# A streaming encoder step on one core: pairwise convolution, tile 0 routed first, its first 16 rows summed by VectorE

## What is computed

```
h = rmsnorm(x); q, k, v, g, a, b = split(h @ w_in)           # six sections of 512 columns
q, k = rotary(q), rotary(k);  o = decayed_retention(q, k, v)  # 4 heads of 128, a state per head
y_ret = silu(g) * normalise(o) * gain
u = a * sigmoid(b); c = depthwise_conv(u, 31 taps) + bias     # 512 channels, over time
y_conv = silu(layernorm(c))
x = x + concat(y_ret, y_conv) @ w_out
h = rmsnorm(x)                                                # then, for each of 8 heads:
scores = (h @ query_head) @ keys      # two halves of 128 keys; top 16 of each, top 16 of the 256 sums
act = gelu(h . down[expert]);  x += sum over 16 experts of softmax * act * up[expert]
y = rmsnorm(x)
```

## Time and profile before

| | us |
|---|---|
| median of 3 runs | 1797.5 |
| the runs | 1796.53, 1797.82, 1797.5 |
| the profiled execution, time | 1796.54 |
| its span, first to last instruction | 1794.6 |
| TensorE, mean granted clock | 0.945 |

### The profile page before, as it was taken

How to read it: one execution, slowest core, us unless ns; L and a number is a source line. 1 busy time by engine, 2 the same in 40 slices (tenths; PEclk the granted TensorE clock), 3 DMA queues, 4 the chain that set the end, 5 groups by cost and what they waited for, 6 DMA issues and landing times.

```text
span 1794.6 us, 14135 instructions
## 1 busy us (share of the span) xinstructions
PE 1522.6 (85%) x4008; PEld 700.3 (39%) x4008; DVE 1171.6 (65%) x2667; ACT 496.4 (28%) x1562; POOL 744.8 (42%) x654
## 2 busy tenths in 40 slices
PE   7999979968988978997798889788977988777887
PEld 3544345534433433342244334333423443332332
DVE  2089863357567767766766777677677677777655
ACT  1000110122332333332333323333333332333332
POOL 1002144133254545453554544444454445455452
PEclk9899989989999999998999999999999999899899
DMA  5112100288999999999999999999999999999996
GB/s 221 47 58 83 62 1 1 68 341 329 362 404 421 421 421 421 422 421 422 421 402 423 422 420 401 422 421 389 408 422 421 421 421 422 421 421 410 421 416 248
DMA packets 84847, 605.53 MB, mean 337 GB/s; under 512 B 10880, under 2 KB 11136, under 8 KB 13088
## 3 DMA queue, kind: packets, MB, share of 16 engines
q0 software_dynamic: 78336, 570.46, 77.1%
q1 hardware_dynamic: 6432, 34.16, 5.0%
HBM read 601.31 MB, written 2.88 MB: 337 GB/s over the span
## 4 chain that ended last, share of the span: by engine, by line
DMA 39%; PE 38%; DVE 13%; ACT 4%; issue 2%; POOL 1%; DVEq 1%; ACTq 1%; POOLq 0%; SPq 0%
DMA arena<-experts,expert 38%; PE ps L1246 21%; DVE region_b L728 6%; PE ps L1217 5%; PE ps L1090 5%; DVE arena L933 5%; PE ps L1077 3%; ACT weight L623 2%; ACT diag L630 1%; PE ps L1082 1%; PE ps L1189 1%; POOL arena L465 1%; PE ps L1104 1%; ACT gl L620 1%; ACTq L625 1%
## 5 line engine op out<-in xcount | busy, mean ns | idle before, releaser
L1246 PE MATMUL ps<-arena,diag 128*128 128x512 f32 x2176 | 1031.2, 631 | 234.1 <-ACT diag L630 233.9
L465 POOL DMA_INDIRECT arena<-experts,expert x544 | 669.3, 1230 | 760.3 <-PE ps L1246 672.4
L933 DVE CUSTOM_DVE_ANT_0 arena<-arena,hn 128x1024 f32<-128x1024 f32 x544 | 654.8, 1222 | 365.9 <-DMA arena<-experts,expert 361.4
L1246 PEld LDWEIGHTS ps<-arena,diag 128*128 128x128 f32 x2176 | 428.8, 201 | 818.9 <-issue 603.4
L620 ACT ACTIVATE gl<-dots 128x4 f32<-128x4 f32 x136 | 27.9, 205 | 801.4 <-DVE dots L933 801.4
L630 ACT ACTIVATE diag<-cst,weight 128x128 f32<-128x128 f32 x544 | 173.8, 390 | 9.6 <-issue 0.3
L1090 PE MATMUL ps<-arena,hT 128*128 128x512 f32 (+1 forms) x320 | 145.9, 616 | 1.0 <-issue 1.0
L623 ACT ACTIVATE weight<-gl,gate 128x1 f32<-128x1 f32 x544 | 115.8, 283 | 9.9 <-issue 0.7
L728 DVE SCALAR_TENSOR_TENSOR region_b<-region_b,par 128x512 f32<-128x512 f32 x240 | 108.0, 521 | 2.7 <-issue 0.5
L1217 PE MATMUL ps<-hT,region_b 128*128 128x512 f32 x224 | 98.5, 593 | 0.4 <-issue 0.4
L441 POOL TENSOR_TENSOR hn<-arena,cst 128x256 f32<-128x256 f32 (+1 forms) x20 | 16.2, 808 | 193.5 <-ACT arena L529 127.0
(11 more groups left out here) (125 smaller groups left out, 845.1 us busy)
## 6 DMA issues: line engine op xcount, KB each, us to landing
arena<-weights SPq DMA_DIRECT2D x8, 2048.0 KB, 8.9
region_b<-head_weights SPq DMA_DIRECT2D x8, 1152.0 KB, 9.4
arena<-experts,expert POOLq DMA_INDIRECT x544, 14.9
xs<-x_prompt SPq DMA_DIRECT2D x4, 512.0 KB, 5.2
y_prompt<-xs SPq DMA_DIRECT2D x4, 512.0 KB, 4.1
cst<-consts SPq DMA_DIRECT2D x1, 836.0 KB, 12.4
region_b<-gain_ffn SPq DMA_DIRECT2D x1, 512.0 KB, 3.7
region_b<-gain_final SPq DMA_DIRECT2D x1, 512.0 KB, 11.5
```

Of the source, the lines that this page charges most:

```text
L465: pool.indirect_dma_start(rows_of(n), None, experts, bass.IndirectOffsetOnAxis(ap=expert[:, vt % BUFS, k:k + 1], axis=0))\
L933: last = v.tensor_tensor_reduce(out=rows_of(n)[:, 0:D], in0=rows_of(n)[:, 0:D], in1=hn[:, tile_of(vt)], scale=1.0, scalar=0.0, op0=ALU.mul ...
L1246: last = mm(ps[:, 2 * (vt % 2) + half, :], diag[:, n % DIAGS, :], rows_of(n)[:, D + half * SEC:D + (half + 1) * SEC], start=k == 0, stop=k ...
```

## The change

Three things are changed. None changes what is computed.

*The convolution by pairs of channel groups.* Prompt and sample columns of a channel group now lie in one row (`EXT` = 604 columns: pad, 512, state of 30, 32), so one instruction covers 574 columns. VectorE does GLU and 31 taps for groups 0 and 1, then for 2 and 3, with two instructions and a drain a tap. TensorE forms the GLU in halves of 272 columns (prompt and sample together), the groups of the first pair first; it begins when three tiles are turned.

*One list, tile 0 first.* `plan()` replaces the two lists and the loops ahead of them. The gate of tile 0 is formed before the channel mean, the other gate tiles and v behind it; layer norm goes in blocks of columns 0 to 128 and 128 to 544; `mix_out`, turn, query and keys of tile 0 come before the retention of tiles 2 to 4 is done. ScalarE evacuates the transposes of q and k and the transposes back. `gate_tanh` has four buffers. GpSimd rotates in place, q and k in one pass of 512 columns, and only behind the last tap. PSUM has eight banks in rotation up to `ffn_t(0, 0)`, and from there banks 4 to 7. SyncE's waits are for products of TensorE instead of a drain behind a section; tile 0's gain has a place of its own.

*The first 16 rows summed by VectorE.* For head tile 0 ScalarE forms only the weights, no diagonals; VectorE adds weight times the `up` half of each row to x (`sum_here`), 16 instructions of 128x1024, each with a drain. Slots get an order of their own (`SLOT`, `PLACE`) for the first 15 gathers: gathers 7 to 10 reuse the slots of 0 to 3, and 11 to 14 take the last weight slots. From gather 26 on each waits for n - 11 as before.

The diff, cut to its core:

```diff
-    for t in range(1, TILES + 1):
-        order += head(t) + out(t - 1) + mid.get(t, []) + scores(t) + back(t - 1) + end.get(t, [])
+    late = [(c, i) for c in (2, 3) for i in range(2)]
+    order = turn("norm_t", 0) + turn("norm_t", 1) + turn("norm_t", 2) + glu(S_A, (0, 0), (1, 0)) + turn("norm_t", 3)
+    order += turn("norm_t", SAMPLE) + glu(S_A, (0, 1), (1, 1)) + glu(S_B, (0, 0), (0, 1), (1, 0), (1, 1))
+    order += glu(S_A, *late) + glu(S_B, *late) + rows(S_Q, *range(TILES)) + rows(S_K, *range(TILES)) + rows(S_G, 0)
+    order += blocks("ln_mean") + rows(S_G, 1) + blocks("ln_var") + rows(S_G, 2, 3, SAMPLE)
+    order += rows(S_V, 0) + head(0) + rows(S_V, 1) + scores(0) + head(1) + out(0) + rows(S_V, 2) + scores(1) + back(0)
+    order += mix(0, 0) + out(1) + head(2) + mix(0, 1) + scores(2) + back(1) + rows(S_V, 3) + turn("ffn_t", 0)
+    order += query(0) + keys(0) + out(2) + head(3) + rows(S_V, SAMPLE) + scores(3) + mix(1, 0) + back(2) + mix(1, 1)
+    order += out(3) + head(4) + scores(4) + turn("ffn_t", 1) + query(1) + keys(1) + back(3) + out(4) + mix(2, 0)
+    order += back(4) + mix(2, 1) + mix(3, 0) + turn("ffn_t", 2) + query(2) + mix(3, 1)
+    order += keys(2) + mix(4, 0) + turn("ffn_t", 3) + query(3) + mix(4, 1) + keys(3)
+    return order + turn("ffn_t", 4) + query(4) + sums(1, 0) + keys(4) + sums(1, 1)
...
-BANKS = 7
+BANKS = 8
+SUM_BANKS = 4
+FIRST_SUM = JOB[("ffn_t", 0, 0)]
+BANK = {name: n % BANKS if n < FIRST_SUM else SUM_BANKS + (n - FIRST_SUM) % (BANKS - SUM_BANKS)
+        for name, n in JOB.items()}
+OPENING = [0, 1, 2, 3, 4, 5, 6, 0, 1, 2, 3, 7, 8, 9, 10]
+CYCLE = [4, 5, 6, 0, 1, 2, 3, 7, 8, 9, 10]
+SLOT = OPENING + [CYCLE[n % SLOTS] for n in range(VT * TOPK - len(OPENING))]
...
+            x_rows(0)
             sp.dma_start(cst[:, C_IDENT:], consts[:, C_IDENT:]).then_inc(s_ident, 16)
             sp.dma_start(par[:, :], params).then_inc(s_par, 16)
+            x_rows(1)
+            x_rows(2)
+            weight_rows(S_A)
...
+            sp.wait_ge(s_pe, JOB[("glu", S_A, CT - 1, 1)] + 1)
+            weight_rows(S_K)
+            sp.wait_ge(s_pe, JOB[("glu", S_B, CT - 1, 1)] + 1)
+            weight_rows(S_G)
+            sp.wait_ge(s_pe, JOB[("qkvg", S_Q, SAMPLE)] + 1)
+            weight_rows(S_V)
...
+            pool.wait_ge(s_conv, 1)
+            rotary(0)
+            decayed_keys(0)
+            for t in range(1, TILES):
+                rotary(t)
...
             mixed_root(0)
+            pool.wait_ge(s_idx, 1)
+            pool.wait_ge(s_pe, JOB[("ret_yT", 1)] + 1)
+            gathers(0, 0, 2)
+            retention_root(2)
+            decayed_keys(3)
+            pool.wait_ge(s_pe, JOB[("qkvg", S_V, SAMPLE)] + 1)
+            gathers(0, 2, 4)
+            pool.wait_ge(s_pe, JOB[("ret_yT", 2)] + 1)
+            gathers(0, 4, 5)
             mixed_root(1)
+            retention_root(3)
+            decayed_keys(4)
+            pool.wait_ge(s_pe, JOB[("ret_yT", 3)] + 1)
+            gathers(0, 5, 6)
+            retention_root(4)
+            pool.wait_ge(s_pe, JOB[("ret_yT", 4)] + 1)
+            gathers(0, 6, 7)
             mixed_root(2)
+            gathers(0, 7, 11)
             mixed_root(3)
+            pool.wait_ge(s_pe, JOB[("mix_out", SAMPLE, 0)] + 1)
+            gathers(0, 11, 13)
+            pool.wait_ge(s_pe, JOB[("mix_out", SAMPLE, 1)] + 1)
+            gathers(0, 13, TOPK)
             mixed_root(SAMPLE)
...
+            for first in range(0, CT, 2):
+                glu(first)
+                last = glu(first + 1)
...
+                for j in range(TAPS):
+                    for c in (first, first + 1):
+                        last = tap(c, j)
+                    if j < TAPS - 1:
+                        dve.drain()
+            last.then_inc(s_conv, 1)
...
+            def sum_here(g):
+
+                for k in range(g * GROUP, (g + 1) * GROUP):
+                    dve.wait_ge(s_diag, k + 1)
+                    v.scalar_tensor_tensor(out=xs[:, 0], in0=rows_of(k)[:, D:2 * D], scalar=weight[:, 0, k:k + 1],
+                                           in1=xs[:, 0], op0=ALU.mult, op1=ALU.add).then_inc(s_used, 1)
+                    dve.drain()
+                if g == GROUPS - 1:
+                    dve.drain().then_inc(s_acc, 1)
...
+            top_sums(0)
+            ret_out(2)
+            ret_state(2)
+            ret_scores(3)
+            mix_add(1, 0)
+            mix_add(1, 1)
+            ret_out(3)
+            ret_state(3)
+            ret_scores(4)
+            dve.wait_ge(s_gain, 16)
             peer_norm(1)
             first_scores(1)
             top_first(1)
+            ret_out(4)
+            ret_state(4)
+            top_second(1)
+            mix_add(2, 0)
+            top_sums(1)
+            mix_add(2, 1)
+
+            gate_scales(0)
+            weigh(0, 0)
+            mix_add(3, 0)
             peer_norm(2)
             mix_add(3, 1)
+            sum_here(0)
+            weigh(0, 1)
             first_scores(2)
             top_first(2)
+            mix_add(4, 0)
+            peer_norm(3)
+            weigh(0, 2)
+            sum_here(1)
             top_second(2)
+            mix_add(4, 1)
             top_sums(2)
             weigh(0, 3)
+            sum_here(2)
+            peer_norm(4)
+            first_scores(3)
 
             gate_scales(1)
             weigh(1, 0)
-            first_scores(3)
+            sum_here(3)
             top_first(3)
             weigh(1, 1)
-            add(0)
```

760 lines of the change are left out of this document (401 added, 359 removed).

## The result

The changed kernel takes 1781.95 us (median of five runs, 1780.23 to 1785.97) against 1796.5 us for the kernel before, timed in the same rounds: a ratio of 0.9924, with the interval 0.9907 to 0.994. The change is worth about 14 us. The prediction said 1756.5 and a range of 1744 to 1777, so it had the sign right and was 25 us too fast, outside its range. The profiled execution took 1783.14 us for a span of 1781.3.

The account below looks back on a forecast made before the run. The prediction took a front until the first later_query, then a DMA-bound stretch of constant length, as the bound: 419 + 1334.5 = 1753.5 us span, 1755.5 executed, forecast 1756.5, range 1744 to 1777.

Parts of the forecast that it names:

- the mark: Start of TensorE's first later_query, behind which the order is unchanged: forecast to move from 460.1 to 419, 41 us earlier.
- Start and GLU: Kernel's start: first GLU product at about 14.5 instead of 19.1, both sections done at 75.0 instead of 94.6.
- Convolution, Q, K, gate: Up to the channel mean: half taps of 1.60 us, taps done at 148.8, mean starting at 151.0 instead of 211.1.
- The layer norm's cover: VectorE's layer norm beside GpSimd's rotations hides: conv_silu(1) ends at 198 to 201, before ret_scores(0) wants VectorE at 201.9.
- 151 to 256: TensorE without long gaps from the channel mean: keys(0) ends at 246.1, expert of tile 0 ready at 256.4 instead of 352.9.
- The stall at v of the sample tile: TensorE idles from 249.7 to 262.1 for VectorE's normalising of ret_out(2), then a slow product of 9.6 us.
- VectorE's sums: Tile 0's 16 row sums on VectorE: 1.40 us each, 5.6 a group, bounds 1.2 and 2.0.
- The constant stretch: From the first later_query to the end: 1334.5 us kept, with the DMA engines full.
- (a): Rival: more waits behind VectorE than counted, first later_query at 429 to 443, 1767 to 1780 us; chance 0.23.
- (b): Rival: fewer waits, TensorE keeping 2.4 GHz across gaps or landings early, 1744 to 1750 us; chance 0.12.
- (c): Rival: VectorE and GpSimd block each other through 256 to 408, 53 us more, 1810 us; chance 0.04.
- (d): Rival: gain absorbed because the stretch behind the first later_query grows, about 1797 us; chance 0.02.

Follow-up runs that it names:

- e1: Changed kernel with VectorE evacuating the transposes of x tile 2 before normalising tile 3: 1779.43 us, ratio 0.9890.
- e6: Changed kernel with the convolution's channel tiles not taken in pairs, a drain behind each tap: 1790.62 us, ratio 0.9963.
- e15: Kernel before the change with 16 of the convolution's 31 taps, so its result differs: 1794.27 us, ratio 0.9992.
- e12: Changed kernel with TensorE's four long waits filled by 13, 7, 22 and 10 products that nobody reads: 1776.36 us, ratio 0.9891.
- e7: Changed kernel with VectorE's 16 sums of tile 0 cut to 16 of 1024 columns, output incomplete: 1780.28 us, ratio 0.9907.
- e14: e11 with VectorE's 16 sums of tile 0 cut to 16 of 1024 columns, output incomplete: 1744.28 us, ratio 0.9718.
- e10: Changed kernel with mix_out(4,1) ahead of the turn of tile 3 in TensorE's order: 1779.23 us, ratio 0.9904.
- e2: Changed kernel with VectorE emptying the bank of the sample tile's scores early, right behind weigh(1,1): 1771.88 us, ratio 0.9859.
- e11: Changed kernel with the edits of e1, e2, e3 and e10 together: 1754.57 us, ratio 0.9766.
- e13: e11 with three of TensorE's remaining waits filled by 4, 2 and 16 products that nobody reads: 1754.38 us, ratio 0.9781.
- e3: Changed kernel with TensorE computing v of the sample tile right behind keys(0), ahead of ret_out(2): 1777.11 us, ratio 0.9890.

## Why the prediction was wrong, step by step

Most terms were right, and three steps failed: the first GLU product (5.3 us late, since a normalisation was priced without the landing of its input), `weigh(0,3)` (8.4 us for 4.6, priced by its instructions and not by the landing of its rows), and the mark (9.2 us, taken to follow the sum although it also waits for a copy of VectorE's). Most of the rest is TensorE at the low clock. The 25 us at the mark, by the point of the prediction at which they arise:

| stretch | forecast | measured | late by | new |
|---|---|---|---|---|
| first GLU product | 14.5 | 19.8 | 5.3 | 5.3 |
| GLU sections end | 75.0 | 83.5 | 8.5 | 3.2 |
| turn of tile 3 starts | 358.8 | 370.0 | 11.2 | 2.7 |
| `weigh(0,3)` ends | 383.9 | 399.8 | 15.9 | 4.7 |
| `weigh(1,1)` ends | 408.0 | 425.4 | 17.4 | 1.5 |
| `sum_up(1,1)` ends | 418.5 | 434.3 | 15.8 | -1.6 |
| first `later_query` | 419.0 | 444.0 | 25.0 | 9.2 |

*Start and GLU: the first step that failed.* "the third tile's rows were normalised at 10.5; two normalisations now stand between the evacuations." The second of them, `normed(3)`, works on rows that are now loaded behind the 2 MB of the first section. They land near 15.6, and VectorE, which takes its orders in turn, waits for them with the turn of tile 2 behind:

```profile
17.77 0.75 DVE L806 TENSOR_SCALAR hn<-xs,rstd 128x1024 f32<-128x1024 f32 x1 [4.42 <-POOL rstd L438]
18.44 1.28 DVE L816 TENSOR_TENSOR hT<-ps,par 128x512 f32<-128x512 f32 x2
```

(VectorE's timeline of the changed kernel.) The forecast had costed the normalisation at its own 0.75 us and not asked when its input lands. e1 puts the product at 14.68, the forecast's 14.5. Behind it, "No 32-column run is left, so I take no clock loss" failed too: the first two products took 10.09 us for 7.4, the granted clock being 0.50 from 20.0 to 24.2. The wait is not the whole reason: in e1, with a wait of 0.79 us, they still took 9.23, at a granted clock that the profile gives as 1.00. The size of a product was right (3.69 each later on).

*Convolution, Q, K, gate: right.* A half tap was 1.615 us (60 instructions in 48.46) for 1.60; the taps ended at 156.4, late only by their start. The mean started at 159.7, 8.7 late and still TensorE's. e6 confirms the 2 to 3 us of slack, e15 that a faster convolution alone was worth next to nothing before.

*The layer norm's cover: held.* `conv_silu(1)` ended at 206.5, 46.8 us behind the mean's start; forecast 47 to 50, and TensorE did not wait for it. VectorE's multiply of 512 columns (L900) took 1.76 us, where one of 574 columns with nothing beside it takes 0.76 (L834): 1 us more, as the sum took. GpSimd's rotation passes of 512 columns took 1.26 for the 1.04 of the forecast, but they did so from 156.5 to 160.8 as well, where VectorE stood still: that is their own length, and beside VectorE single ones grew to 1.72. The Trainium skill (page "SBUF — State Buffer", section "Who interferes with whom") has a VectorE instruction with two SBUF inputs contend with a GpSimd instruction that reads SBUF, and the grown instructions agree. The 58 us that the prediction drew from it, with nothing of the two overlapping, did not come: the measurement lies 11 under that.

*151 to 256: right.* `keys(0)` ended at 255.4 for 246.1, its route at 265.8 for 256.4, late by what had been lost before and under 1 us more.

*The stall at v of the sample tile: right*, gap 12.5 and product 9.97, 9.4 late like its surroundings. The later low-clock stretches were counted too short: from the turn of tile 1 to `keys(1)` 9.1 us for 7.9, turn and query of tile 3 8.3 for 7.2. The slow sum was `sum_up(1,0)` (8.90) and not `sum_up(1,1)` (7.13 for the forecast's 8.8), which is the -1.6 of the table. What the low clock costs behind four of these waits is the 5.6 us of e12.

*VectorE's sums: size right, price wrong.* 1.38 us apart (forecast 1.40). But the step "from here VectorE alone: ... `weigh(0,3)` 4.6" is wrong: three of its four rows go out only at 385.5 to 388.0, because `mix_out(4,1)` ends at 385.2, and its last three dot products start 2.5 to 2.9 us apart, at the pace of the DMA engines. It took 8.4 us. That a dot product costs 2.5 us when its row is the last thing to come was in the transfers' rate and their size, and the forecast used neither for a tile whose gathers are issued late. e7 shows it from one side, e14 from the other, e10 that part of it comes back.

*The mark: the step that is missing.* "`sum_up(1,1)` at 409.7 ..., mark at 419" takes `later_query` to follow the sum. It also waits for the bank of the last `scores`, which VectorE empties behind the whole route of tile 3 and the landings of `weigh(1, 2)`. That order is in both kernels. Before, VectorE reached the copy early and itself waited for TensorE's product (VectorE's timeline of the kernel before), so that TensorE's next step at 460.06 showed no gap:

```profile
459.73 0.23 DVE L866 COPY region_b<-ps 128x64 f32<-128x64 f32 x1 [1.93 <-PE ps L1180]
```

e2 removes the gap and the DMA hole, 10 us of median.

*The constant stretch: right in kind.* 1337.3 for 1334.5; with the hole gone, 1334.1 (e2).

Among the rivals, (a), more waits behind VectorE, was the case in kind, but not for most of the terms given to it (taps and sums had their size, only the clock was as it said), and the time lies past its end, in the band from 1780 to 1793 that had 4 in a hundred. (b), (c) and (d) did not happen: through 256 to 408 VectorE's dot products took 1.20 to 1.23 us and four sums 5.41, so nothing on its path grew by a factor of 1.6, and the gain was not absorbed behind the mark. None of the three signs of being wrong showed beyond what was counted either (taps ended at 156.4, VectorE's instructions grew only in the layer norm, the stretch was 1337.3): they watched the terms that held, and none watched a wait. e11 and e13 come near the forecast time, but that is luck and no proof of it: two of e11's four edits (e3, e10) mend what the forecast had taken as it was.
